# A two-layer transformer with a routed expert layer: first gather cut to 32 columns, 1.5 MB of expert weights moved to earlier places in the queue, splits and last blocks reordered

## The reference

```python
def expert_block(args):
    xb, e = args
    hid = jax.nn.silu(xb @ w1[e]) * (xb @ w3[e])
    return hid @ w2[e]
...
x = x + hier_moe(rms_norm(x, g_ffn), w_group, b_group, w_expert, b_expert, w1, w3, w2)
return rms_norm(x, g_final)
```

## Time and profile before

| | |
|---|---|
| median of 3 runs | 1076.07 us (1074.75 to 1076.33) |
| profiled execution | 1076.97 us, of which the span is 1074.9 |
| PE busy | 932.0 us, 87% of the span |
| DVE busy | 505.0 us, 47% |
| ACT busy | 364.1 us, 34% |
| DMA, mean | 288 GB/s, 310.00 MB |
| mean granted TensorE clock | 0.951 of full |

### The profile page before, as it was taken

One profiled execution on the slowest core, in us unless ns is written; L12 is line 12 of the kernel. 1 busy time (PEld: TensorE's weight loads), 2 busy tenths in 40 slices (PEclk: granted clock), 3 DMA queues, 4 the chain that ended last, 5 costly groups with the idle time before them and its releaser, 6 DMA issues.

```text
span 1074.9 us, 22614 instructions
## 1 busy us (share of the span) xinstructions
PE 932.0 (87%) x9976; PEld 767.0 (71%) x9976; DVE 505.0 (47%) x812; ACT 364.1 (34%) x517; POOL 32.6 (3%) x34
## 2 busy tenths in 40 slices
PE   9999999999999999999999988886766657676754
PEld 8998877888888888989777876665545546464642
DVE  5647768687676667889877651110000100010101
ACT  6445766454444345444666330000000000000001
POOL 1200002110000001000000000000000000000000
PEclk9999999999999999999999999998888988797988
DMA  9954434545555654444457999999999999999995
GB/s 330 309 176 165 152 130 163 172 162 196 195 183 169 211 160 157 158 157 157 158 180 285 392 399 425 422 427 426 427 426 429 428 429 429 429 429 429 428 429 209
DMA packets 86830, 310.00 MB, mean 288 GB/s; under 512 B 5612, under 2 KB 46264, under 8 KB 73976
## 3 DMA queue, kind: packets, MB, share of 16 engines
q1 hardware_dynamic: 84816, 304.20, 73.4%
q0 software_dynamic: 1056, 4.20, 1.2%
q10 hardware_dynamic: 904, 0.81, 0.2%
HBM read 308.15 MB, written 1.05 MB: 288 GB/s over the span
## 4 chain that ended last, share of the span: by engine, by line
PE 58%; issue 38%; DVE 2%; ACT 1%; POOL 1%; ACTq 0%; POOLq 0%; DVEq 0%
PE ps L879 13%; PE ps L881 12%; PE ps L880 12%; PE ps L1003 7%; PE ps L1005 4%; PE ps L1358 1%; PE ps L1152 1%; PE ps L1374 1%; PE ps L1140 1%; PE ps L1058 1%; ACT x_both L1582 1%; PE ps L1302 0%; PE ps L1064 0%; POOL stat L816 0%; PE ps L978 0%
## 5 line engine op out<-in xcount | busy, mean ns | idle before, releaser
L1358 PE MATMUL ps<-arena,xg 128*32 128x128 f32 x2816 | 108.9, 318 | 75.1 <-DMA arena<-in_w 72.7
L1742 DVE TENSOR_TENSOR w_split<-arena,w_split 128x2048 fp32r<-128x2048 f32 x70 | 159.3, 2287 | 28.3 <-ACT w_split L1419 27.8
L2328 DVE TENSOR_TENSOR hid<-silu_e,ps 128x128 f32<-128x128 f32 x32 | 12.1, 378 | 313.6 <-ACT silu_e L1691 313.6
L1358 PEld LDWEIGHTS ps<-arena,xg 128*32 128x32 f32 x2816 | 93.4, 128 | 92.5 <-DMA arena<-in_w 86.0
L1419 ACT ACTIVATE w_split<-arena 128x2048 fp32r<-128x2048 f32 x70 | 132.7, 1900 | 66.1 <-PE ps L881 57.9
L1003 PE MATMUL ps<-x_both,w_split 128*128 128x512 f32 x352 | 124.8, 398 | 0.0
L879 PE MATMUL ps<-w_split,x_both 128*128 128x512 f32 x256 | 102.2, 399 | 0.3 <-DVE w_split L1798 0.3
L880 PE MATMUL ps<-w_split,x_both 128*128 128x512 f32 x256 | 99.8, 390 | 0.0
L881 PE MATMUL ps<-w_split,x_both 128*128 128x512 f32 x256 | 99.8, 390 | 0.0
L1005 PE MATMUL ps<-x_both,w_split 128*128 128x256 f32 x352 | 98.8, 281 | 0.0
L1374 PE MATMUL ps<-arena,hid_T 128*32 128x256 f32 x960 | 68.0, 428 | 28.1 <-DMA arena<-in_w 26.9
(11 more groups left out here) (325 smaller groups left out, 1471.4 us busy)
## 6 DMA issues: line engine op xcount, KB each, us to landing
arena<-in_w SPq DMA_DIRECT2D x71, 2048.0 KB, 26.0
arena<-in_w_in SPq DMA_DIRECT2D x41, 1024.0 KB, 5.1
even_w<-in_w SPq DMA_DIRECT2D x13, 2048.0 KB, 26.4
arena<-in_w_ffn_in SPq DMA_DIRECT2D x22, 1024.0 KB, 5.1
third_w<-in_w SPq DMA_DIRECT2D x6, 2048.0 KB, 16.6
arena<-in_w_ffn_out SPq DMA_DIRECT2D x11, 1024.0 KB, 4.9
arena<-in_w_out SPq DMA_DIRECT2D x8, 1024.0 KB, 6.4
arena<-in_w SPq DMA_DIRECT2D x6, 1024.0 KB, 7.5
```

Source lines behind the costliest of these rows:

```text
L1358: last = mm(ps[SLOTS * g:SLOTS * g + SLOTS, 6, P * n:P * n + P], xg[:, c, SLOTS * e:SLOTS * e + SLOTS], places[n][:, c, P * g:P * g + P], ...
L1742: v.tensor_tensor(w_lo[:, u % 3, 0:n], ring[:, u % 3, 0:n], w_hi[:, u % 3, 0:n].bitcast(F32), ALU.subtract).then_inc(lo_ready, 1)
L2328: v.tensor_tensor(hid[:, :].rearrange("p (b i) -> p i b", b=4), silu_e[:, :].rearrange("p (i b) -> p i b", b=4), ps[:, 6, P:2 * P].rearran ...
```

## The change

- *Gather.* Only in the first quad: PE first gathers the 32 columns of expert 0, does w1 of expert 0, then gathers the other 96 columns, then w3 of expert 0. The copies of `xg` on ACT and DVE are cut in the same way. `CHOICE_WARM` goes from 10 to 14.
- *Loads ahead.* The first half (1 MB) of w3 of expert 1 is loaded in the dense part, behind unit `kiwi`+7, after a wait of SP for `rope_done` 4. A quarter (0.5 MB) of w2 of expert 3 gets a buffer of its own (`spare_w2`, room for which is made by laying `gate_e` over `masked_e`) and is issued before w3 of expert 3; the other three quarters stand where w2 of 3 stood.
- *Last down matrix.* In the loop, now over quads, w2 of each quad's last expert comes as three quarters and one quarter, each with a semaphore.
- *Start.* Both halves of unit 0 are loaded before the second half of the tokens; PE turns that half before chunk 1 and not before chunk 2. The DVE split of unit 2 is two instructions.
- *Second residual.* DVE splits `kiwi`+1 before it waits for the squares.
- *Last blocks.* Means and roots for one block of 128 tokens at a time, block 1 first; ACT scales columns 0 to 511 of each block, DVE the others; SP issues all four stores.

```diff
-CHOICE_WARM = 10
+CHOICE_WARM = 14
...
-                if u == 0:
-                    cols = slice(512 * half, 512 * half + 512)
-                    sp.dma_start(h[:, :, cols], x_v[:, :, cols]).then_inc(in_x[half], 16)
+                if (u, half) in ((0, 0), (1, 0)):
+                    cols = slice(512 * u, 512 * u + 512)
+                    sp.dma_start(h[:, :, cols], x_v[:, :, cols]).then_inc(in_x[u], 16)
...
+        def odd_half(half):
+            part = slice(4 * half, 4 * half + 4)
+            sp.dma_start(odd_w[1][:, part, :], sources[1][:, 1, part, :]).then_inc((odd_first, landed_w[1][1])[half], 16)
...
             load(u)
+            if u == first["kiwi"] + 7:
+                sp.wait_ge(rope_done, 4)
+                odd_half(0)
...
         sp.wait_ge(lo_ready, U - 2)
-        expert_load(1, odd_w, 1, landed_w[1][1])
+        odd_half(1)
...
         expert_load(2, third_w, 2, in_third3[2])
+        sp.dma_start(spare_w2[:, :], sources[2][:, 3, 0, :]).then_inc(spare_in, 16)
...
         sp.wait_ge(e_y, 1)
-        expert_load(3, fourth_w, 2, in_fourth[2])
+        sp.dma_start(fourth_w[2][:, 1:4, :], sources[2][:, 3, 1:4, :]).then_inc(in_fourth[2], 16)
...
+                        if (j, which) == (QUAD - 1, 2):
+                            src = sources[2][:, bass.ds(e, 1), :, :].rearrange("p e c n -> p (e c) n")
+                            sp.dma_start(odd_w[2][:, 0:3, :], src[:, 0:3, :]).then_inc(landed_w[1][2], 16)
+                            sp.dma_start(odd_w[2][:, 3:4, :], src[:, 3:4, :]).then_inc(last_block, 16)
...
-                    if c == 2:
+                    if c == 1:
                         turn_tokens(1)
...
+            def collect(lo, hi):
+                for half in range(2):
+                    for tb in range(TB):
+                        if half == 0:
+                            pe.wait_ge(hot_part, q * 2 + (tb + 1))
+                        for i in range(4):
+                            last = mm(ps[:, 4 + half, P * i + lo:P * i + hi], n3g[:, tb, 4 * half + i, :],
+                                      one_hot[:, tb, lo:hi], start=tb == 0 and i == 0, stop=tb == 1 and i == 3)
+                    last.then_inc((xg_half, xg_done)[half], 1)
+            collect(0, SLOTS if first_quad else P)
...
                     last.then_inc((e_w1, e_up)[n], 1)
+                    if first_quad and (e, n) == (0, 0):
+                        collect(SLOTS, P)
...
+                    if looped and (e, b) == (QUAD - 1, 3):
+                        pe.wait_ge(last_block, pe.snap(q * 16 - 16))
...
+            if n:
+                split(G0 + 3 * NF + 1)
             dve.wait_ge(sq_done, n + 3)
             mean_square(norm_event[n + 2])
-            split((G0, G0 + 3 * NF)[n] + 1)
+            if not n:
+                split(G0 + 1)
...
+        for n, (i, tb) in enumerate(((0, 1), (0, 0), (1, 0))):
...
+        for n, tb in enumerate((1, 0)):
+            act.wait_ge(root_last, n + 1)
+            act.wait_ge(fin_gain, n + 1)
+            part = n3[:, tb, 0:512]
+            fn(part, part, ACT.Copy, scale=stat[:, last_event, 6 + tb:7 + tb]).then_inc(fin_act, 1)
```

More of the change, by code:

```diff
@@ L444, in layers_kernel @@
     chosen = moe("chosen", [P, TB, EXPERTS])
[L445 removed]
+    gate_e = moe("gate_e", [P, TB, EXPERTS], where=masked_at)
     rank = moe("rank", [P, TB, EXPERTS])
@@ L558, in layers_kernel @@
     seeded, logit_part = sem("residual_seeded"), sem("logit_part")
-    sq_low, sq_all, last_kept = sem("final_sq_low"), sem("final_sq_all"), sem("final_kept")
+    sq_last, last_kept, mean_last, root_last = (sem(f"final_{n}") for n in ("square", "kept", "mean", "root"))
     comb_done = sem("comb_done")
     fin_gain, fin_out = sem("final_gain"), sem("final_out")
-    fin_ready = [[sem(f"final_ready{tb}{i}") for i in range(2)] for tb in range(TB)]
+    fin_act, fin_dve = sem("final_ready_act"), sem("final_ready_dve")
     def landings(u):
@@ L779, in _, with stream @@
             expert_load(7, odd_w, which, landed_w[1][which])
[L781 to L786, removed]
+        def stream(pass_, lo_quad):
+            with sp.Fori(lo_quad, EXPERTS // QUAD) as i:
+                for j in range(QUAD):
+                    e = sp.snap(i * QUAD + j)
+                    used = sp.snap(i * QUAD + (pass_ * EXPERTS + j - 1))
                     for which in range(3):
                         sp.wait_ge((e_w1, e_up, e_y)[which], used)
-                        expert_load(e, (even_w, odd_w)[odd], which, landed_w[odd][which])
-        stream(0, 4)
+                        if (j, which) == (QUAD - 1, 2):
+                            src = sources[2][:, bass.ds(e, 1), :, :].rearrange("p e c n -> p (e c) n")
+                            sp.dma_start(odd_w[2][:, 0:3, :], src[:, 0:3, :]).then_inc(landed_w[1][2], 16)
+                            sp.dma_start(odd_w[2][:, 3:4, :], src[:, 3:4, :]).then_inc(last_block, 16)
+                        else:
+                            expert_load(e, (even_w, odd_w)[j % 2], which, landed_w[j % 2][which])
+        stream(0, 2)
         sp.wait_ge(passes_ready, 1)
@@ L797, in _ @@
             sp.nop()
-        for i in (1, 0):
-            sp.wait_ge(fin_ready[1][i], 1)
+        for tb, i in ((1, 0), (1, 1), (0, 0), (0, 1)):
+            sp.wait_ge((fin_act, fin_dve)[i], 2 - tb)
             cols = slice(512 * i, 512 * i + 512)
-            sp.dma_start(out[0, P:T, cols], n3[:, 1, cols]).then_inc(fin_out, 16)
+            sp.dma_start(out[0, P * tb:P * tb + P, cols], n3[:, tb, cols]).then_inc(fin_out, 16)
         sp.wait_ge(fin_out, 64)
@@ L1296, in quad_body @@
                 pe.wait_ge(n3_ready, 2)
-            for half in range(2):
-                for tb in range(TB):
-                    if half == 0:
-                        pe.wait_ge(hot_part, q * 2 + (tb + 1))
-                    for i in range(4):
-                        last = mm(ps[:, 4 + half, P * i:P * i + P], n3g[:, tb, 4 * half + i, :], one_hot[:, tb, :],
-                                  start=tb == 0 and i == 0, stop=tb == 1 and i == 3)
-                if half == 0:
-                    last.then_inc(xg_half, 1)
-            last.then_inc(xg_done, 1)
+            first_quad = not looped and q == 0
+            def collect(lo, hi):
[8 more added lines that the diff above has]
+            collect(0, SLOTS if first_quad else P)
             def place_of(e):
@@ L1363, in quad_body @@
                     last.then_inc((e_w1, e_up)[n], 1)
+                    if first_quad and (e, n) == (0, 0):
+                        collect(SLOTS, P)
+                if e == 0 and first_quad:
+                    for half in range(2):
+                        pe.wait_ge((xg_part, xg_ready)[half], 2)
                 if e == 0:
```

86 lines of the change are left out of this document (53 added, 33 removed).

## The result

The changed kernel takes 1087.22 us (four runs, 1085.29 to 1092.06) against 1076.2 before: 1.0113 times as long, 95% interval 1.0094 to 1.0132. The forecast was 1072.3 and its range ended at 1075.4. The profiled execution took 1088.32 us with a span of 1086.4.

The account below looks back on a forecast made before the run. PE bounds the kernel up to routing, then bytes left at DMA saturation and earlier DMA idling, then the tail. Terms -0.8 - 0.7 - 1.4 - 0.9 = -3.8 from 1076.07 gave 1072.3 us; 8-in-10 range 1069.2 to 1075.4.

Parts of the forecast that it names:

- DMA queue: -1.4: Transfers from the first gather on: fewer bytes in the saturated stretch, less new idle gaps; -1.4 us, bounds -4.5 to +0.5.
- rival 2: First gather cheap by its columns, 0.9 us and 2.75 for the second, no queue gap; 1069.2 us, chance 0.10.
- rival 4: Slower: second gather and low clock delay PE through the first quad, w2 of expert 4 starves; 1080.6 us, chance 0.08.
- credit for the preload: Saturated stretch: of the 1.5 MB loaded ahead, 1 MB of w3 leaves it, -2.46 us; 0.5 MB fills the former gap.
- Rival 3: Queue gives everything back through a gap at `e_y` 4, and the tail gives nothing; 1074.6 us, chance 0.18.
- Start: Dense part's first units: ACT's transfer wait goes and PE's two waits shrink; -0.8 us, bounds 0.3 and 1.1.
- residual: PE's 0.71 us wait for the split of `kiwi`+1 goes; -0.7 us, bounds 0.5 and 0.8.
- tail: Kernel's end: divided last w2 saves 0.7 us and earlier stores 0.2; -0.9 us in all.
- the late item that the prediction named: At the start, the inverse root behind the first row sum was expected to be late next; no separate size.
- SP's new wait: Wait for `rope_done` 4 delays units `kiwi`+8 and +9; cost 0 with 5 us of cover, at most 3.3.
- The clock: First gather: four more warm matmuls shorten PE's idle time to 0.65 us, keeping the clock at 2.4 GHz.
- Rival 1: Clock falls in the gather as before, which then costs 1.5 us more; 1074.1 us, chance 0.17.

Follow-up runs that it names:

- e14: Changed kernel with its first gather in one piece and CHOICE_WARM left at 14; 1073.80 us, ratio 0.9978.
- e12: Changed kernel with CHOICE_WARM 3 in place of 14, so 44 fewer PE instructions ahead of the loop; 1080.55 us, ratio 1.0039.
- e5: Changed kernel with 133 PE instructions that only wait, ahead of PE's loop; 1081.48 us, ratio 1.0057.
- e4: Changed kernel with the first gather in one piece again and 10 warm matmuls; 1073.59 us, ratio 0.9979.
- e1: Kernel before with 82 PE instructions that only wait, ahead of PE's loop; 1085.86 us, ratio 1.0087.
- e11: Kernel before with 41 PE instructions that only wait, ahead of PE's loop; 1075.70 us, ratio 0.9997.
- e6: Changed kernel with one-piece first gather and 10 warm matmuls, without the 1.5 MB loaded ahead; 1074.16 us, ratio 0.9979.
- e8: Changed kernel with one-piece first gather and 10 warm matmuls, order of the start as before; 1073.88 us, ratio 0.9974.
- e7: Changed kernel with one-piece first gather and 10 warm matmuls, each quad's last w2 whole; 1074.05 us, ratio 0.9985.
- e2: Changed kernel with 20 PE instructions that only wait, ahead of PE's loop; 1088.52 us, ratio 1.0114.
- e3: Changed kernel with the last w2 of each quad loaded in one piece again; 1089.72 us, ratio 1.0121.
- e9: Changed kernel with one-piece first gather, 10 warm matmuls and 214 PE instructions that only wait ahead of the loop; 1085.05 us, ratio 1.0083.

## Why the prediction was wrong

The change of +11.0 us falls into three parts: e14 against before, -2.6; the split gather, e12 against e14, +6.8 (e5 against e4, less the 0.7 of its idle instructions, says +7.2); fetching the loop's code, changed kernel against e12, +6.7 (against e5, less the 0.7, +6.4). The border between the last two is good to a few us only: with four and six runs, the difference of changed kernel and e12 has a 95% interval of about 4 to 11.5. That a refetched loop costs 9.65 us in the kernel before (e1) is within it.

1. **Not foreseen at all: the loop's place.** The prediction priced added instructions by PE's time beside other work. It counted 32 for the gather and 8 for warming, and never asked where they push the loop: their effect on the code behind them was put at nothing, without a reason. With e1 and e11 it is shown, on the kernel before, at 9.65 us. None of the four rivals was this one.

2. **The step that failed inside the prediction: "DMA queue: -1.4".** It had PE 2.0 us later than before at `e_y` 4 and a last gap of 0.7 us there. On the clock of the kernel before PE was 5.6 us late, and a larger gap came behind that point. The gathers were forecast at 3.2 and 3.5 and took 4.09 and 3.81; e5 shows 3.73 for 32 columns at clock 1.00. The claim that columns hardly matter was right, and rival 2, with 0.9 us, was wrong: e4's gather of 128 columns takes 3.81. (Rival 2 took a quarter of the price for a quarter of the columns, while the rule that it was to stand for gives a half; e5 shows neither.)

   The forecast's times were on the clock of the kernel before, and the changed kernel reached routing 1.2 us earlier (last logits at 623.81, before 625.02), so 1.2 must be added to its times. Then `e_w1_half` came at 637.4 (forecast 636.0), `e_up` at 644.3 (642.15) and `e_y` 4 at 676.0 (672.4): 1.4, 2.2 and 3.6 us late. That the printed times, 636.24 and 643.12, look like the forecast is luck. The first 2.2 are about the longer gathers (0.9 and 0.3) and w1 at the low clock (3.20 for 2.00). The other 1.4 lie between `e_up` and `e_y` 4: PE took 1.8 us longer there than before, where the forecast had added 0.3 for stalls, and its "issue" waits in this stretch sum to 6.3 us, before to 2.8. They change from kernel to kernel (2.8 in e4, 5.7 in e14, 5.3 in e5), so part of this is where the code's blocks end, and which part no run settles.

   The losses by the rate (GB/s short of 426, times 5 us) are 2.1 us at 635, 1.5 at 640, 0.6 at 645 and 0.8 at 650 (374 and 362 GB/s), 0.9 at 675, 3.0 at 690 and 0.5 at 695, in sum 9.4 against 3.35 forecast (1.9 before, forecast as 2.0). In the sum of the forecast this makes the queue term -2.46 - 1.9 + 9.4 = +5.0 and not -1.4. The largest loss is one the prediction didn't look for. It stopped at `e_y` 4, but behind it stands w1 of expert 7, which waits for the sixth w1 to be used, and that came 5.3 us later than before. So rival 4 had the right quad and direction, though w2 of expert 4, which it named, lost only 0.9 us. It was given 0.08 because a queue 3.1 us in hand was taken as safe. That its 1080.6, meant for all four experts at 1.2 GHz, is what e12 measures is luck.

3. **The credit for the preload was too large.** 1 MB was to give 2.46 us less the gaps. With one gather it gave 0.6 (e6 against e4, not clear of zero). A shorter queue runs dry sooner while PE's releases come no earlier: from 635 to 640 e4 has 338 GB/s, e6, without the preload, 378, which is 0.5 us. Rival 3 described that; where the rest of the 2.46 went stays open.

4. **Start, residual and tail were right in direction by the traces.** In time, taking back the start (e8) cost 0.3 us and taking back the divided w2 (e7) 0.5, neither clear of zero; the residual and the order of the last blocks were not run alone. PE waited neither the 0.39 and 0.69 us of rows 7 nor the 0.71 of rows 8. A new wait of 0.98 us for `p_tok` at 21.80 took back most of the start. It isn't the late item that the prediction named: POOL's inverse root ended at 17.60, and ACT began `p_tok` at 20.99, behind the rounding of a unit for whose transfer it had waited 1.82 us. The last logits were reached at 623.81, before at 625.02: -1.2 for a forecast of -1.5, though e5 and e12, with the same code up to there, have 624.86 and 625.35, so this is hardly above the scatter. From the last landing to the end of the span it is 11.4 us, before 12.5: -1.1 for a forecast of -0.9. No wait of PE for a split came from SP's new wait.

5. **The clock.** It was forecast at 1.00 from 630 to 641; it was 0.86, 0.50 and 0.79 in the three stretches of 2 us from 632. The low stretch did not go away with less idle time but moved: it lay on the gather before (5.30), on w1 in the changed kernel (3.20), and on the warm matmuls in e4, where PE has time. In e14 it doesn't appear from 620 to 640, and e14 takes as long as e4. Rival 1 was right that the clock falls, though it fell on w1 and not on the gather. With one gather that is worth nothing measurable (e4, e8, e14); with the split it was 1.2 us of `e_up`'s lateness, and its price alone was not measured.

## What to carry to other kernels

Before adding instructions on an engine, look at which loops stand behind them in its program: count the blocks of code that a loop touches, and watch the row of code packets; a loop that runs without fetching is an asset that 82 instructions ahead of it destroyed here, while 41 did nothing. A loss of that kind shows as "issue" waits at the head of each turn and as a DMA share of 0.5 at the very end, and it is told from the work's own cost by moving the loop and changing nothing else. And where a release is made later, follow the queue not to the first transfer that has time in hand but through all that wait on the same engine behind it.

## What the runs showed of the hardware

- A loop of PE of 1612 to 1614 instructions ran without any code fetch or with 9 packets of 16 KB in each turn, depending on its place alone (e11 and e1). The Trainium skill, page "Runtime: NRT & Kernel Launch", section "Instruction fetch mechanics", also calls the instruction memory "only 2 cache lines" of 16 KiB; for PE the runs disagree, since the code of a turn, over 6 such blocks, was kept from the loop's first turn through its sixth.
- Nine packets, 0.15 MB, in a turn of 60 us are 0.6% of the bytes. They cost more than their bytes, because one packet puts one landing back by about 1.5 us, and the delays fall on the same eight of 16 landings and mostly stay (in e1 the spread fell once, from 12.8 to 10.4 near 1043 us): from 780 to 1040 us, 4.4 turns, the spread grew from 3.3 to 11.0 us, 1.75 a turn. An estimate from these rows: in the four kernels that refetch (changed, e1, e2, e3), the 16 lags grew by 1.1 to 1.6 us in sum for each packet, so the 46 further packets, shared by eight engines, are 6 to 9 us, which is what the runs measure (6.4 to 9.65).
- Code fetched once leaves a spread too: before, 1.9 us near 640 and 4.9 near 780.
- 214 PE instructions that each wait for a semaphore already reached took 22.5 us (e9), 133 took 13.8 (e5): 0.105 and 0.104 each, beyond a code block on the way.
- A gather matmul with 32 columns takes as long as one with 128: 32 instructions in 3.73 us (e5) and 3.81 (e4).
